# A two-block transformer kernel on one core: the first norm without waits for constants, bulk constants issued later

## The reference, cut

```
x = h * rsqrt(mean(h*h) + eps) * ln_ffn1            # first norm
h = h + 0.5 * ((silu(x @ w1_gate) * (x @ w1_up)) @ w1_down)
lb  = softmax over two rows of logits               # decay bounds, used in the next stage
ang = positions * inv_freq; cos(ang), sin(ang)      # rotation, used in the next stage
mod = c @ w_mod + b_mod                             # modulation of the second block
```

## Time and profile before

| | |
|---|---|
| median of 3 runs | 1628.04 us (1626.09 to 1629.92) |
| profiled execution | 1627.11 us, its span 1625.3 us |
| outside the span | 1.8 us |
| busy: PE, DVE, POOL, ACT | 1420.8, 989.0, 711.1, 556.8 us |
| mean granted clock of PE | 0.959 of full speed |

### The profile page before, as it was taken

The page is one execution under the profiler, slowest core; times in us unless marked ns, Lnnn a source line. Parts: engine busy times, 40 slices in busy tenths (PEclk is TensorE's granted clock), DMA queues, the critical chain, the costliest instruction groups (busy, mean ns, idle before and its releaser), DMA issues.

```text
span 1625.3 us, 21353 instructions
## 1 busy us (share of the span) xinstructions
PE 1420.8 (87%) x8186; PEld 1086.8 (67%) x8186; DVE 989.0 (61%) x1779; ACT 556.8 (34%) x936; POOL 711.1 (44%) x442
## 2 busy tenths in 40 slices
PE   8999899998999899999999888778777777777886
PEld 8999899978999898899888773333333333333332
DVE  5788423555786624622543648777777777777653
ACT  4434345424444334544343432222222222222211
POOL 2434346402344444396575466444434443444430
PEclk9999999999999999999999999999999999899988
DMA  7776554303577453143333369999999999999993
GB/s 312 262 265 218 184 181 151 104 27 126 210 260 257 162 201 114 63 163 131 104 105 130 121 230 413 420 420 421 420 421 420 421 420 420 420 421 420 420 420 134
DMA packets 59206, 427.16 MB, mean 263 GB/s; under 512 B 6576, under 2 KB 6896, under 8 KB 7792
## 3 DMA queue, kind: packets, MB, share of 16 engines
q0 software_dynamic: 36864, 268.45, 39.9%
q1 hardware_dynamic: 20736, 149.96, 26.1%
q10 hardware_dynamic: 1520, 7.60, 1.2%
HBM read 424.93 MB, written 1.05 MB: 262 GB/s over the span
## 4 chain that ended last, share of the span: by engine, by line
PE 38%; DMA 28%; DVE 15%; issue 8%; POOL 5%; ACT 5%; ACTq 0%; DVEq 0%; POOLq 0%; SPq 0%
DMA keys<-in_expert_uv,arena 21%; PE ps L413 6%; PE ps L418 6%; PE ps L414 5%; DMA rows_x<-in_expert_uv,arena 5%; POOL wlo L319 5%; PE ps L834 4%; PE ps L835 4%; PE ps L488 2%; PE ps L490 2%; PE ps L489 2%; DMA ring<-in_w 2%; DVE arena L1274 2%; DVE arena L1589 2%; ACT whi L901 1%
## 5 line engine op out<-in xcount | busy, mean ns | idle before, releaser
L319 POOL TENSOR_TENSOR wlo<-ring,whi 128x1024 fp32r<-128x1024 f32 x162 | 409.9, 2539 | 513.0 <-ACT whi L901 512.6
L413 PE MATMUL ps<-nh,whi 128*128 128x256 f32 x1440 | 364.9, 290 | 11.8 <-ACT nh L915 6.0
L901 ACT ACTIVATE whi<-ring 128x1024 fp32r<-128x1024 f32 x236 | 243.8, 1054 | 355.1 <-PE ps L418 163.5
L414 PE MATMUL ps<-nh,wlo 128*128 128x256 f32 x1440 | 356.7, 284 | 0.0
L413 PEld LDWEIGHTS ps<-nh,whi 128*128 128x128 f32 x1440 | 277.4, 193 | 18.0 <-issue 5.9
L414 PEld LDWEIGHTS ps<-nh,wlo 128*128 128x128 f32 x1440 | 278.0, 193 | 0.3
L418 PE MATMUL ps<-nl,whi 128*128 128x256 f32 x1440 | 207.1, 286 | 0.0
L319 DVE TENSOR_TENSOR wlo<-ring,whi 128x1024 fp32r<-128x1024 f32 x74 | 106.8, 1454 | 138.3 <-ACT whi L901 132.6
L418 PEld LDWEIGHTS ps<-nl,whi 128*128 128x128 f32 x1440 | 188.4, 193 | 2.5 <-DVE nl L1221 0.5
L1712 POOL DMA_INDIRECT arena<-in_expert_uv,arena x96 | 109.5, 1140 | 152.9 <-PE ps L835 139.8
L1589 DVE CUSTOM_DVE_ANT_0 arena<-arena 128x1024 f32<-128x1024 f32 x96 | 122.4, 1275 | 44.7 <-DMA arena<-in_expert_uv,arena 40.6
(11 more groups left out here) (303 smaller groups left out, 2383.4 us busy)
## 6 DMA issues: line engine op xcount, KB each, us to landing
ring<-in_w SPq DMA_DIRECT2D x118, 1024.0 KB, 4.9
arena<-in_wmod SPq DMA_DIRECT2D x24, 1024.0 KB, 5.0
small<-in_small ACTq DMA_DIRECT2D x1, 2816.0 KB, 19.6
arena<-in_expert_uv,arena POOLq DMA_INDIRECT x96, 26.5
h<-in_x ACTq DMA_DIRECT2D x1, 1024.0 KB, 8.0
keys<-in_keys ACTq DMA_DIRECT2D x1, 1024.0 KB, 26.1
rows_w<-in_expert_uv,arena POOLq DMA_INDIRECT x64, 25.5
out<-h SPq DMA_DIRECT2D x2, 512.0 KB
```

What stands on the lines that cost most here:

```text
L319: return v.tensor_tensor(wlo[:, tile % TILES, :], ring[:, tile // 2 % RAW, at:at + TILE], whi[:, tile % TILES, :].bitcast(F32), ALU.subtract)
L413: mm(to, hi[:, k, :], nh[:, k, :], start=(k == 0), stop=False)
L414: mm(to, lo[:, k, :], nh[:, k, :], start=False, stop=False)
L901: fn(whi[:, tile % TILES, :], ring[:, slot % RAW, at:at + TILE], ACT.Copy).then_inc(S("high_w"), 1)
```

## The change

`con` counts on a semaphore of its own. The first norm waits for `x` and `vec` alone. PE waits for `con` after the first stage, and DVE before the angles. A root of one element stands on ACT ahead of the squares. The fillers around the first sum are 26 and 12 instead of 44 and 24. ACT issues the six larger transfers behind the norm's copies. DVE's L1227 to L1238 become `angles`, its L1244 to L1251 `bounds`, each behind one of the first two `weighted`; ACT's exponential and sines come behind its second `gate`.

```diff
             pe.wait_ge(S("constants"), 2)
-            keep_busy(44, bank=5)
-            pe.wait_ge(S("vec_landed"), 32)
+            keep_busy(26, bank=5)
             for c in range(C):
                 square_sum(0, c)
-            keep_busy(24, bank=5)
+            keep_busy(12, bank=5)
             swiglu(S_FFN1, 0, 0, 1, 0)
+            pe.wait_ge(S("con_landed"), 16)
...
-            act.dma_start(con[:, :], a["con"]).then_inc(S("vec_landed"), 16)
+            act.dma_start(con[:, :], a["con"]).then_inc(S("con_landed"), 16)
...
-            act.dma_start(wf[:, :, :], a["wf"]).then_inc(S("small_landed"), 16)
...
+            def load_rest():
+                act.dma_start(wf[:, :, :], a["wf"]).then_inc(S("small_landed"), 16)
...
             act.wait_ge(S("constants"), 2)
+            fn(std[:, 1, 0:1], eps[:, 0:1], ACT.Sqrt)
             for c in range(C):
                 square(0, c)
             while tile < 2:
                 high(tile)
                 tile += 1
-            act.wait_ge(S("lb_shifted"), 1)
-            fn(lb[:, 2:4, :], lb[:, 0:2, :], ACT.Exp).then_inc(S("lb_exp"), 1)
-            act.wait_ge(S("angle"), 1)
-            own(fn(sin[:, :], ang[:, 0, :], ACT.Sin))
-            fn(cos[:, :], ang[:, 0, :], ACT.Sin, scale=0.5).then_inc(S("sines"), 1)
             root(0)
             high_norm(0)
+            load_rest()
+            def bounds_and_sines():
+                act.wait_ge(S("lb_shifted"), 1)
+                fn(lb[:, 2:4, :], lb[:, 0:2, :], ACT.Exp).then_inc(S("lb_exp"), 1)
+                act.wait_ge(S("angle"), 1)
+                own(fn(sin[:, :], ang[:, 0, :], ACT.Sin))
+                fn(cos[:, :], ang[:, 0, :], ACT.Sin, scale=0.5).then_inc(S("sines"), 1)
...
                 gate(n, 0, before)
                 gate(n + 2, 1, before)
+                if before == 0:
+                    bounds_and_sines()
...
-            dve.wait_ge(S("vec_landed"), 32)
...
             low(v, dve, 0).then_inc(S("low_dve"), 1)
             tile = 2
+            dve.wait_ge(S("vec_landed"), 16)
             norm(0, V("ffn1", 0, C), sq, "normed")
             low_x(0)
+            def angles():
+                rows = V("lb", 0, 2 * HH).rearrange("p (r h) -> p r h", r=2)
...
+                dve.wait_ge(S("pos_landed"), 16)
+                dve.wait_ge(S("con_landed"), 16)
+                own(v.tensor_copy(ang[:, 1, :], posi[:, :]))
...
+            def bounds():
+                dve.wait_ge(S("sines"), 1)
+                own(v.tensor_tensor(ang[:, 2, :], cos[:, :], cos[:, :], ALU.mult))
...
                 for b in range(2):
                     gated(n + 2 * b, b, before)
                     weighted(mod + b, pairs)
+                    if mod == 0:
+                        (angles, bounds)[b]()
```

More of the change, by code:

```diff
@@ L848, in _ @@
             act.dma_start(vec[:, :], a["vec"]).then_inc(S("vec_landed"), 16)
-            act.dma_start(con[:, :], a["con"]).then_inc(S("vec_landed"), 16)
+            act.dma_start(con[:, :], a["con"]).then_inc(S("con_landed"), 16)
             act.dma_start(posi[:, :], a["pos"].partition_broadcast(ROPE).rearrange("p a t -> p (a t)")
                           ).then_inc(S("pos_landed"), 16)
-            act.dma_start(wf[:, :, :], a["wf"]).then_inc(S("small_landed"), 16)
[L853 to L859, removed]
+            def load_rest():
+                act.dma_start(wf[:, :, :], a["wf"]).then_inc(S("small_landed"), 16)
+                act.dma_start(small[:, :], a["small"]).then_inc(S("small_landed"), 16)
+                act.dma_start(lev_mask[:, :, :], a["lev_mask"]).then_inc(S("small_landed"), 16)
+                act.dma_start(inv_count[:, :, :].rearrange("p g t -> p (g t)"),
+                              a["inv_count"].partition_broadcast(P).rearrange("p a t -> p (a t)")
+                              ).then_inc(S("small_landed"), 16)
+                act.dma_start(keys[:, :, :], a["keys"]).then_inc(S("small_landed"), 16)
+                act.dma_start(pT[:, :, :], a["p"]).then_inc(S("p_landed"), 16)
             def square(m, c):
@@ L1249, in _ @@
-            own(v.reciprocal(lb[:, 5, :], lb[:, 4, :]))
-            own(v.tensor_tensor(lb[:, 0, :], lb[:, 2, :], lb[:, 5, :], ALU.mult))
-            own(v.tensor_scalar(lb[:, 1, :], lb[:, 0, :], -1.0, 1.0, ALU.mult, ALU.add))
+            def angles():
+                rows = V("lb", 0, 2 * HH).rearrange("p (r h) -> p r h", r=2)
+                own(v.tensor_tensor(lb[:, 4, :], rows[:, 0, :], rows[:, 1, :], ALU.max))
+                v.tensor_tensor(lb[:, 0:2, :], rows, over(lb[:, 4, :], 2), ALU.subtract).then_inc(S("lb_shifted"), 1)
+                dve.wait_ge(S("pos_landed"), 16)
+                dve.wait_ge(S("con_landed"), 16)
+                own(v.tensor_copy(ang[:, 1, :], posi[:, :]))
+                own(v.tensor_scalar(ang[:, 0, :], ang[:, 1, :], K("inv_freq", ROPE), None, ALU.mult))
+                own(v.tensor_scalar(ang[:, 1, :], ang[:, 0, :], TURN_INV, None, ALU.mult))
+                own(v.tensor_scalar(ang[:, 2, :], ang[:, 1, :], ROUND, None, ALU.add))
+                own(v.tensor_scalar(ang[:, 1, :], ang[:, 2, :], ROUND, None, ALU.subtract))
+                for part in TURN:
+                    own(v.scalar_tensor_tensor(ang[:, 0, :], ang[:, 1, :], -part, ang[:, 0, :], ALU.mult, ALU.add))
+                v.tensor_scalar(ang[:, 0, :], ang[:, 0, :], HALF_TURN, -HALF_TURN, ALU.min, ALU.max
+                                ).then_inc(S("angle"), 1)
@@ new lines, in bounds @@
+            def bounds():
+                dve.wait_ge(S("sines"), 1)
+                own(v.tensor_tensor(ang[:, 2, :], cos[:, :], cos[:, :], ALU.mult))
+                own(v.tensor_scalar(cos[:, :], ang[:, 2, :], -2.0, 1.0, ALU.mult, ALU.add))
+                dve.wait_ge(S("lb_exp"), 1)
+                own(v.tensor_tensor(lb[:, 4, :], lb[:, 2, :], lb[:, 3, :], ALU.add))
+                own(v.reciprocal(lb[:, 5, :], lb[:, 4, :]))
+                own(v.tensor_tensor(lb[:, 0, :], lb[:, 2, :], lb[:, 5, :], ALU.mult))
+                own(v.tensor_scalar(lb[:, 1, :], lb[:, 0, :], -1.0, 1.0, ALU.mult, ALU.add))
```

## The result

The changed kernel took 1631.71 us (median of 9 runs, 1630.28 to 1633.3), the kernel before 1628.04 beside it (9 runs, 1625.32 to 1630.94): a ratio of 1.0024, 95% interval 1.0013 to 1.0035, or 3.7 us more. The profiled execution has a span of 1630.8 and took 1632.57.

The account below looks back on a forecast made before the run. No engine bounds the whole chain; behind the head start, slot 3 and DVE's chain set tile 8. Terms -5.5 + 3.6 + 2.2 + 1.7 = +2.0 us gave 1629.5 us, range 1622.5 to 1633.5.

Parts of the forecast that it names:

- rival A: Start of tile 8: the full sum, two POOL blocks and the clock's fall, +2.0 us (0.5 to 3.2); chance 0.42.
- D: Slot 3: bulk goes ahead of the weights, landing at 38.5, +4.4 us, 1632 to 1633; chance 0.20.
- -5.5 for the low part of tile 6: DVE before tile 8: slot 3 lands at 36.15, so tile 6's low part ends 5.5 us earlier, at 38.6.
- Head start: First norm: without the wait for `con`, angles and table loads, PE's first product starts 8.9 us earlier, at 17.1.
- The six issues took from 2.92 to 6.05: ACT behind the norm's copies: issues assumed as long as before, from 19.7, leaving ACT free at 22.8.
- Slot 3's landing: SP's queue: a slot loaded against bulk takes 8.8 us, so slot 3 lands at 36.15; bounds 6.07 and 38.5.
- an estimate of a sum 1.25 smaller: Slot 3 beside the bulk: sharing by packets gives it 3.75 us of flow instead of 5; not adopted.
- Angles and the second block: DVE before tile 8's low part: angles add 3.6 us, a second block by POOL 2.2 us.
- The clock: PE after some 10 us of wait before tile 8: half speed for 3.4 us costs 1.7 us.
- Bounds and sines: zero: DVE and ACT around tile 12: later bounds, exponential, sines and three table loads cost zero, up to 2 us if POOL blocks.
- C: Start of tile 8: the head start is kept, 8.9 us off, 1619; chance 0.18.
- B: DVE before tile 8: one POOL block only, -0.2 or -2.9 us, 1625 to 1628; chance 0.20.

Follow-up runs that it names:

- kernel 4: Changed kernel, four bulk transfers issued behind the second gate's sines, keys and pT behind the second norm, angles in DVE's wait before tile 6: 1623.04 us.
- Kernel 11: Changed kernel, ACT splits tiles 2 and 3 before its six bulk issues: 1626.25 us.
- kernel 3: Changed kernel with only the angles moved, into DVE's wait before tile 6: 1628.15 us.
- kernel 7: Changed kernel, all six bulk transfers issued at the start and angles in DVE's wait before tile 6: 1621.76 us.
- kernel 8: Changed kernel, DVE computes the angles twice in the same place: 1634.9 us.
- kernel 10: Changed kernel with PE filler calls in its early waits, 10 before tile 6 and 40 before tile 8: 1630.13 us.
- kernel 9: kernel 7 plus DVE's low part of tile 8 ahead of the first modulation sum: 1628.57 us.
- kernel 12: Changed kernel, bulk first, low part of tile 8 before the first modulation sum, angles, bounds and sines in the down projection: 1625.79 us.
- kernel 5: Changed kernel with PE filler calls in its early waits, 10 before tile 6 and 32 before tile 8: 1628.99 us.
- kernel 6: Changed kernel, four bulk transfers issued at the start, keys and pT behind the second norm, angles in DVE's wait before tile 6: 1625.61 us.
- kernel 2: Changed kernel, four bulk transfers issued behind the second gate's sines, keys and pT behind the second norm's copies: 1626.4 us.

## Why the prediction was right, and where it was off

It said 1629.5, within 1622.5 to 1633.5; it was 1631.71. The mechanism is the one of rival A: the head start runs into the ring, DVE's chain holds tile 8, and the clock falls behind the wait. The size, +3.7, lies between A (0.5 to 3.2) and D (+4.4). It is also just above the 3.3 us that I took for the smallest visible change, so it falls to "slower", which had a chance of 0.25, and not to "within", which had 0.55. The term of the sum that was mis-sized is the first, -5.5 for the low part of tile 6: it was -3.1.

**Head start.** Forecast 8.9, measured 9.5. The reciprocal ran its 1.75 us at 13.59, in the middle of a POOL row (13.21, 2.44 us), so it isn't kept waiting, as the earlier trace rows had suggested. Neither the early root nor the smaller number of fillers cost anything.

**The issues.** "The six issues took from 2.92 to 6.05" did not carry over: from 18.74 they took 4.9 us, and slot 3 was issued at 28.3 instead of 27.35. PE also waited 1.34 us before tile 2, where I had no wait. Busy transfers do not explain the longer issues: the DMA share was 0.97 from 2.92 to 6.05 and 0.92 from 18.74 to 23.62, and in kernel 4 the first four, issued from 48.73 at a share of 1.01, took 1.8 us, for 2.1 at the start and 3.3 in the kernel after. The cause stays open. Kernel 11 shows the term at work: 3.6 us of slot 3.

**Slot 3's landing.** Forecast 8.8, measured 10.4. D's sign, a landing after 37.5, was met (38.7), but not its mechanism: the bulk had not gone wholly ahead: `keys` and `pT` landed at about 41 and 44. The modulation block behind slot 3 took 13.1 us, slot 4 12.6. The row of 8.8 was not "the same mix": slot 2 had SP's queue to itself, slot 3 had the modulation block right behind it (issued at 28.71). Packets, MB and share of the DMA engines from issue to landing, by queue (q10 is ACT's with the bulk, q1 is SP's), for slot 2 of the kernel before (21.59 to 30.40) and then slot 3 of the kernel after (28.33 to 38.69):

```profile
q10 hardware_dynamic: 564, 2.35, 65.5%
q1 hardware_dynamic: 144, 1.05, 28.5%
```

```profile
q10 hardware_dynamic: 519, 2.43, 62.1%
q1 hardware_dynamic: 207, 1.56, 36.8%
```

The bulk took about the same part of both, 2.4 MB; SP's queue moved 0.5 MB more than the slot. At the mean rate of both stretches, 387 GB/s, the 0.6 MB between the two sums make 1.55 us, the difference of the landings (an estimate; no run takes the modulation block away). Without bulk beside it, in kernel 4, slot 3 was split 5.0 us after its issue. The Trainium skill ("DMA: Bandwidth & Descriptors", Queues, rings and completion order) would share by packets; I had worked out from it an estimate of a sum 1.25 smaller, for the case that `small` with its rows of 22 KB was through. It landed at about 30, 1.8 us behind slot 3's issue, and the slot came later than in the row of 8.8 all the same. No run here shows shares of single packets.

Together these two put the low part of tile 6 at 41.03, 3.1 us earlier than before and not 5.5. That is the whole miss, and more.

**Angles and the second block.** Forecast 3.6 and 2.2; the angles ran from 49.89 to 55.42, 5.5 us, of it 2.0 the block on L1248, in the place and of the kind forecast. Kernels 3, 7 and 8 show the price by taking them out and doubling them.

**The clock.** Forecast 1.7, measured 1.54 (3.74 at tile 9, 2.19 at tile 8), and 1.5 by kernel 10. Unforeseen was an earlier fall, behind 3.27 us of wait before tile 6: PE ran at 0.50 there, and it cost nothing, since the wait before tile 8 lay behind it. I had said that there would be no wait before tile 6. My own numbers did not give that: PE through with tile 5 at 36.6 and the low part of tile 6 at 38.6 make a wait of 2 us, and the late slot 3 made it 3.27.

**Bounds and sines: zero.** Right for this kernel. DVE's bounds ran unblocked. But I had counted three table loads in all, and there are more: one ahead of the split after the sines, and then two in each later turn of the loop that goes on with the tiles. ACT's rows at the sines, and its groups of table loads at the splits and at `silu`, kernel after:

```profile
62.37 0.42 ACT L943 ACTIVATE cos<-arena 64x256 f32<-64x256 f32 x1
62.95 1.28 ACT L904 ACT_TABLE_LOAD   x1 [0.17 <-issue]
```

```profile
L904 ACT ACT_TABLE_LOAD x4 | 5.1, 1283 | 8.7 <-DMA ring<-in_w 8.5 <-issue 0.2
L950 ACT ACT_TABLE_LOAD x6 | 7.7, 1283 | 0.1
```

The kernel before has none at its splits and two at `silu` (L944). The loads at the splits are at 62.95, 86.89, 110.71 and 134.88, the last three between a slot's landing and its split. PE does not wait from tile 9 to tile 43, so all of them were hidden here. In a kernel that is ahead they need not be: in kernel 9 the chain runs through both loads of the second turn (85.4 and 88.7) to a wait of 1.60 us before tile 24. No run takes them away alone; kernel 12, with the sines in the down projection, has none at its splits.

The sum at tile 12 is +3.74 for a forecast of +2.0: -3.1 (low part of tile 6), +5.3 (from there to tile 8: 15.65 us for 10.38, the angles and their block less 0.2 in the modulation sum), +1.5 (clock). The medians say +3.7. The rivals: C (head start kept) was refused by slot 3 and DVE's chain; kernel 4, with both put elsewhere, keeps it at tile 8. B (one block) didn't come: the second POOL row was there, at 50.67.

**What stays open.** In the profiled execution the difference grows from 3.73 at 166.02, the start of the down projection, to 5.06 at 175.57 and ends at 5.5, though the change touches nothing there; the medians, 3.7 apart, don't carry it. Slots land at other times in each execution (PE waits 3.57 us before 175.57, where the earlier trace rows have 2.24), and granted clocks of 0.50 follow in other places; I have no experiment on it. Also open is the best order for tiles 8 to 14: kernels 9 and 12 show a further 3 to 4 us at tile 8, and what takes it back.

## To carry to other kernels

Ask of a step that is moved into a free stretch what its engine has to do next, and who waits for that: here six issues of half a microsecond became 4.9 us in front of two splits on which the ring hung; with the same issues at the start, or two splits later, tile 8 came 4.8 and 4.4 us earlier. A function with another table ahead of a loop can put loads into every turn of it. Side work belongs in a queue's real idle time (DVE had 10 us of it before the low part of tile 6), not between a sum and the operand that the bound engine is waiting for. A head start is worth what the next limited resource behind it can take up: trace it through the ring's next slot before counting it.

## What was unexpected of the hardware

- Issuing six transfers from ACT's queue took 4.9 us at 18.74 (0.34 to 1.14 each) and 3.1 us at the start, with transfers flowing in both cases.
- A slot of 1 MB landed 10.4 to 12.6 us after its issue while the bulk flowed; the median over all 118 issues of a slot is 4.9.
- A copy on ACT behind a sine had a table load in front (1.28 us at 62.95), and so had the first copy of every later turn of the loop.
- A `TENSOR_TENSOR` of 128x4 took 2.37 us instead of 0.17 beside POOL (kernel 7, 28.83), and a `RECIPROCAL` of 128x256 its usual 1.75.
- The granted clock, read as a mean over some 3.4 us behind a PE wait, was 0.50 for waits of 3.27 and 7.18 us (after), 0.55 for 2.43 (kernel 5), 0.57 and 0.69 for 2.05 and 1.93 (kernel 6) and 0.69 for 1.71 (kernel 12, 61.06). It stayed at 1.00 behind 1.0 and 1.3 (kernel 10), but also behind 1.85 at 51.19 in kernel 3 and 2.38 at 186.50 in kernel 2. The length of the last wait alone does not tell which it will be.
